# Context row tiles of a PEER layer spread by the steps' times minus the transfer of the weights that they load

## The reference, cut to what matters

```
h  = rmsnorm(x) * (1 + sc1) + sh1
u, v, zb, q, k, rv, rg_f, rg_b, gm = split(h @ w_in)
y_a = gelu(u) * mix128(layernorm(gelu(v)));  y_b = pool(zb) @ pool_w
y_c = silu(rg_f) * headnorm(scan_f(q,k,rv)) + silu(rg_b) * headnorm(scan_b(q,k,rv))
x  = x + gt1 * ((ga*y_a + gb*y_b + gc*y_c) @ w_out)
h2 = rmsnorm(x) * (1 + sc2) + sh2
# PEER: for each token and each of 8 heads, the best 16 of 128 x 128 experts
s1, s2 = (h2 @ wq) . subkeys;  top16 of each side;  top16 of their 256 sums
x  = x + gt2 * sum_experts softmax(score) * gelu(u_tab[e] . h2) * v_tab[e]
y  = rmsnorm(x) * final_norm_g
```

## Time and profile before

| what | value |
|---|---|
| median of 3 runs | 4568.91 us (4568.11 to 4576.76) |
| profiled execution | 4571.26 us, span 4569.5 us |
| TensorE busy, mean granted clock | 3741.4 us (82%), 0.871 |
| VectorE busy | 2791.1 us (61%) |
| DMA | 1672.73 MB, 366 GB/s over the span |
| of it row tiles | 1342.26 MB, 1280 issues |

### The profile page before, as it was taken

How to read it: one execution, slowest core, us unless ns; L and a number is a source line. 1 busy time by engine, 2 the same in 40 slices (tenths; PEclk the granted TensorE clock), 3 DMA queues, 4 the chain that set the end, 5 groups by cost and what they waited for, 6 DMA issues and landing times.

```text
span 4569.5 us, 44582 instructions
## 1 busy us (share of the span) xinstructions
PE 3741.4 (82%) x12065; PEld 1568.4 (34%) x12065; DVE 2791.1 (61%) x6341; ACT 1640.7 (36%) x5133; POOL 1622.7 (36%) x1312
## 2 busy tenths in 40 slices
PE   8999999999998689999776887888777556666666
PEld 6654455656553233443221232342222111011110
DVE  1122776577676976654898566545678984544544
ACT  4211345232213343334344333333343553333333
POOL 0000132223222333333434434443444445555554
PEclk9999999999999799999887998999877676666666
DMA  8645688789999989999999989999999999999998
GB/s 343 228 166 214 261 336 324 272 305 378 373 406 401 366 353 402 382 377 411 398 394 340 420 350 405 400 400 409 401 400 383 395 397 415 413 421 415 415 421 349
DMA packets 277883, 1672.73 MB, mean 366 GB/s; under 512 B 30528, under 2 KB 48000, under 8 KB 91136
## 3 DMA queue, kind: packets, MB, share of 16 engines
q0 software_dynamic: 184320, 1342.26, 73.3%
q1 hardware_dynamic: 85152, 304.18, 17.3%
q10 hardware_dynamic: 8160, 23.43, 1.6%
HBM read 1631.98 MB, written 37.78 MB: 365 GB/s over the span
## 4 chain that ended last, share of the span: by engine, by line
PE 44%; DMA 29%; DVE 14%; issue 7%; ACT 4%; POOL 2%; DVEq 0%; ACTq 0%; SPq 0%; POOLq 0%
DMA slots<-in_peer,idxR 27%; PE ps L1394 27%; PE ps L1412 9%; DVE slots L1701 4%; PE ps L1387 4%; POOL slots L1098 2%; ACT lhs L1153 1%; ACT wgts L1145 1%; DVE ti L1721 1%; DVE ti L1718 1%; DMA counts<-in_mlat 1%; DVE tv L1720 1%; PE ps L1518 1%; DVE rest L1719 1%; ACT gelus L1142 1%
## 5 line engine op out<-in xcount | busy, mean ns | idle before, releaser
L1098 POOL DMA_INDIRECT slots<-in_peer,idxR x1280 | 1616.4, 1263 | 2871.8 <-PE ps L1412 1779.8
L1412 PE MATMUL ps<-slots,lhs 128*64 128x512 f32 x4544 | 1483.1, 767 | 725.2 <-ACT lhs L1153 722.7
L1701 DVE CUSTOM_DVE_ANT_0 slots<-slots,h2R 128x1024 f32<-128x1024 f32 x1280 | 1546.2, 1223 | 763.8 <-issue 706.5
L1394 PE MATMUL ps<-ring,arena 128*128 128x512 f32 (+1 forms) x3264 | 1365.1, 575 | 15.2 <-ACT arena L1353 6.5
L1412 PEld LDWEIGHTS ps<-slots,lhs 128*64 128x64 f32 x4544 | 294.8, 158 | 1811.2 <-ACT lhs L1153 1582.3
L1394 PEld LDWEIGHTS ps<-ring,arena 128*128 128x128 f32 x3264 | 623.2, 195 | 769.8 <-issue 752.3
L1142 ACT ACTIVATE gelus<-dots 128x1 f32<-128x1 f32 x1280 | 256.5, 200 | 1509.6 <-DVE dots L1701 1505.5
L1153 ACT ACTIVATE lhs<-fold,wgts 128x64 f32<-128x64 f32 x1136 | 395.1, 348 | 37.2
L1145 ACT ACTIVATE wgts<-gelus,gsmR 128x1 f32<-128x1 f32 x1280 | 377.2, 295 | 42.4 <-ACT gelus L1142 0.5
L1394 PE MATMUL ps<-ring,slots 128*128 128x512 f32 (+1 forms) x576 | 221.6, 545 | 0.0
L1713 DVE SCALAR_TENSOR_TENSOR slots<-slots,wgts 128x1024 f32<-128x1024 f32 x135 | 172.9, 1281 | 79.0 <-ACT wgts L1145 73.0
(11 more groups left out here) (206 smaller groups left out, 2420.2 us busy)
## 6 DMA issues: line engine op xcount, KB each, us to landing
ring<-in_whead SPq DMA_DIRECT2D x48, 1024.0 KB, 9.6
ring<-in_wa SPq DMA_DIRECT2D x48, 1024.0 KB, 9.2
ring<-in_wq SPq DMA_DIRECT2D x32, 1024.0 KB, 16.2
slots<-in_peer,idxR POOLq DMA_INDIRECT x1280, 13.1
ring<-in_wgc SPq DMA_DIRECT2D x16, 1024.0 KB, 9.5
ring<-in_wgb SPq DMA_DIRECT2D x16, 1024.0 KB, 9.9
ring<-in_wout SPq DMA_DIRECT2D x16, 1024.0 KB, 14.8
o_scratch<-inb SPq DMA_DIRECT2D x80, 128.0 KB, 5.2
```

Of the source, the lines that this page charges most:

```text
L1098: g.indirect_dma_start(out=slot(R), out_offset=None, in_=a["peer"], in_offset=bass.IndirectOffsetOnAxis(ap=idxR[:, p % KEEP, g2, col:col + ...
L1394: done = mm(out, lhsT, rhs, start=n == 0, stop=n == KD - 1)
L1412: done = mm(ps[j * HALF:(j + 1) * HALF, g2, :], weights, slot(R)[:, D + j * UW:D + (j + 1) * UW], start=start, stop=stop)
L1701: v.tensor_tensor_reduce(out=u, in0=u, in1=h2R[:, g2, :], scale=1.0, scalar=0.0, op0=ALU.mult, op1=ALU.add, accum_out=dots[:, R % LHS:R % ...
```

## The change

The weight by which the context's rows (k = 0) are spread is no longer `wall` but `wall` minus 5.3 for each step that starts a weight unit. Groups 1 and 2 keep `wall`, group 3 keeps `spare_time`. The costs of the steps, their order and the number of rows are as before; the rows' places between the steps change, and with them the first row of the chained runs and the row `few` at which slots 6 and 7 come into use.

```diff
         spare = self.spare_time()
+        free = [time - UNIT_TIME * ev.first for time, ev in zip(wall, self.front)]
         due = [0.0] * (len(self.front) + 1)
         for k, cs in enumerate(GROUPS):
             a, b = starts[k], starts[k + 1]
-            weight = spare if k == len(GROUPS) - 1 else wall
+            weight = spare if k == len(GROUPS) - 1 else free if k == 0 else wall
             total = sum(weight[a:b])
             rows = min(len(cs) * ROWS, total / ROW_TIME if k == len(GROUPS) - 1 else len(cs) * ROWS)
```

## The result

The changed kernel takes 4597.62 us (median of 4 runs, 4596.29 to 4605.19) against 4568.51 us before: 29 us more, ratio 1.0067 (95% interval 1.0053 to 1.0080). The forecast was 4566, the range 4552 to 4585: it is wrong, and in the direction of its third rival, which had given 4583.5.

A forecast was written before the change was run, and what follows sets the result against it. It took TensorE to bound most stretches ahead of group 1, VectorE head 3's scans, with DMA near full in group 1; +13.7 ahead and -16.9 in group 1 and after gave -3.2, so 4566 us, range 4552 to 4585.

The forecast's parts named there:

- Rival 3: VectorE becomes the bound ahead of group 1, in ranking, first scans and pools: +14.6 us, 4583.5; chance 0.20.
- Term (a): Ranking: seven more rows at TensorE's 0.98 us, VectorE's cost hidden, +1 for slot refill; 6.8 to 12.1 us.
- Term (d): Scans of head 3: two more rows at 2.5 us, less 2.1 for an eviction moved ahead; +3, 0 to +6.
- Term (g): Group 1's mix and first head gates: chain ends move away, taking 9 of 10 us off; at least 4.
- Term (i): Group 1's transposes and wout: one row fewer saves 1 us (0 to 5); the 4.12 us chain-end wait stays.
- (b): Projections of head 2: 8 rows on TensorE become 10, with no cover; +1.9 us.
- (c): First scan steps of head 2: chained rows, their wait and low clock go, seven TensorE rows come; 0, -2 to +4.
- (f): Group 1's v, u and ga: TensorE is busy 87.93 of 88.2 us, so nothing is saved; 0.
- (h): Group 1's gb: 30.2 us against group 0's 27.4, 0.9 of it a chain end; saves 1.9 (0 to 1.9).
- (j): Query steps of group 1: two rows fewer save 4 us, between 2.0 at TensorE's pace and 5.3 at the DMA engines'.
- (e): Pools: three more rows on VectorE, hidden, and one more chain end on TensorE; +1 us, 7.5 if none hidden.
- Rival 2: Transfers hold back all of group 1, so fewer rows there gain more: -12.5 us, 4556; chance 0.25.

The follow-up runs named there:

- experiment 4: Changed kernel with the dot products of rows 0 to 81 over 512 instead of 1024 elements; 4578.61 us, ratio 1.0028.
- experiment 14: Kernel before with the dot products of rows 0 to 74 over 512 instead of 1024 elements; 4556.58 us, ratio 0.9975.
- experiment 12: Changed kernel with five instead of six slots for the rows up to the end of the ranking; 4608.82 us, ratio 1.0087.
- Experiment 9: Kernel before with 8 rows fewer in the scans of heads 2 and 3 and as many more in the pools; 4570.39 us, ratio 1.0011.
- experiment 10: Kernel before with 63 instead of 75 context rows beside the ranking, the others moved beside heads 2 and 3; 4563.59 us, ratio 0.9992.
- experiment 15: Changed kernel's spread with at most one row in all but one scan step of head 3; 4572.39 us, ratio 1.0014.
- experiment 16: Kernel before with 63 rows beside the ranking, four chain ends taken one row later, and single rows in head 3's scan steps; 4555.88 us, ratio 0.9970.
- experiment 8: Changed kernel with TensorE taking chain ends 175, 191, 207 and 223 one row later; 4587.07 us, ratio 1.0045.
- experiment 6: Kernel before, gathering only the v half of rows 168 to 228, those beside group 1; 4561.83 us, ratio 0.9992.
- experiment 7: Kernel before with TensorE taking chain ends 175, 191, 207 and 223 one row later; 4566.77 us, ratio 0.9999.

## Why the prediction was wrong

**The placement was right, the cost ahead of group 1 was not.** The 60 records, the run that goes back, seven rows beside the ranking and three each beside the later parts all came as worked out (the places from the planner's costs, the records from the trace). The sum ahead of group 1 was +13.7 and is +28 (19.0 ranking, 4.2 head 2, 6.9 head 3, -2 pools); in the second profile it is +32.

**Term (a) failed, by 11 to 13 us.** "VectorE pays 1.30 a row, but is busy 212 of 267 us, which hides it" took an average over two kinds of steps and called its 55 idle us cover. They were none: 17.0 of them are waits for TensorE in the scans between, 19.6 waits for rows to land, and in the ranking's first part VectorE was 94% busy, 67.74 of 72.4 us. What the runs showed in place of the cover: 19.0 to 20.6 us for seven rows, of which 9 to 10 go when half of the dot products is left out on both sides (experiments 4 and 14), and TensorE's idle time in the ranking rises from 11.5 to 20.9 us. Even my upper bound, 12.1, was too low. It charged each row with VectorE's 1.30; it left out that TensorE's wait is followed by slow matmuls (8.76 us for 7.13) and that the six slots come free later, as experiment 12 suggests. Measured, a row is 1.09 us from 63 to 75 rows and 2.7 to 2.9 from 75 to 82. The busy share of the first part alone does not tell the two apart: with 63 rows it is 94% as well (62.86 of 66.7 us). The price of a row is not a constant, and my bounds used one on each side.

**Rival 3 was the right mechanism, with its price too low.** It named the ranking and gave "VectorE's work in a ranking step passes TensorE's 9.8 us" as the point. It had 0.20 because of the "55 us idle", the same average. Its price for the ranking, 12.1, is 8 us below what came; its prices for the first scans and the pools (4 and 7.5) were not paid.

**Term (d): the direction and cause were right, the unit was wrong.** I priced each row that a scan step holds at 2.5 us, less 2.1 for an eviction. Experiment 9 took rows out of head 3's scan steps and gained 0.9, and 4.9 in head 2 where it took away the step with two; experiments 10, 15 and 16 show that a second row in a step is what costs: the wait of 3.51 us and the pair of matmuls at 1.16 us behind it. Three such steps where there had been one gave 6.2 to 8.2; one, as before, gave 0.4.

**Not priced: later scans of head 2 (+3.4) and projections of head 3 (+1).** My list of stretches had a gap from 854.8 to 931.3 us, and what stands there had no term.

**Term (g) was right, and the step behind it missing.** What it said of the two chain ends, "both away from the four evictions of mix", held: -10.0 for -9, and the 6.57 us wait is gone. That the next chain end would land at "the third head gate" was in the text as part of the gain. It cost 6 of the 7 us there: VectorE's last accumulation now stands behind the gate's work and TensorE's use of it one row later, behind the same step. Experiment 8 separates them and has the part at +1.1. I had left the stretch from 1297.2 to 1352.4 out of the sum because before it had no wait.

**Term (i) was wrong in sign, +4 to +9 for -2.** A chain end was foreseen ("a wait of 4.12 us for a chain end stays"); it is 2.71 us. Not foreseen was the wait of 4.85 us, 1.70 before, for an evacuation that now stands behind a table load and a row's gelu. Projections behind these waits take 9.33 and 10.08 us where a clock at full gives some 7.1. The two profiles differ by 5 us here because the clock fell behind the wait of 2.71 in one and not in the other; the size is open to that extent.

**Right: (b), (c), (f), (h), (j).** +2.1 for 1.9, -1.3 for 0, 0 for 0, -2.7 for -1.9, -3.8 and -2.4 for -4. In (c) the mechanism held as well: no wait and no low clock, 20.1 us, all of it busy. The pools (e) gave -2.0 for +1. The carry behind row 256 held within what two profiles of one kernel differ by (3022.7 and 3031.2 around 3025.3).

**Rival 2 and the rule of turns between queues.** Halving the bytes beside group 1 (experiment 6) brought 4.1 us, not the 23.2 of "transfers hold back all of group 1". So rival 2 fell. The forecast had also worked out, from the turns between queues in "DMA: Bandwidth & Descriptors" of the Trainium skill, section "Queues, rings and completion order", that a weight transfer is as late with 47 rows as with 61. That fell too. Group 1's weights in the second profile of the changed kernel (KB each, median us to landing), and one of them before:

```profile
ring<-in_wgb SPq DMA_DIRECT2D x4, 1024.0 KB, 8.2
ring<-in_wout SPq DMA_DIRECT2D x4, 1024.0 KB, 11.4
...
ring<-in_wgb SPq DMA_DIRECT2D x4, 1024.0 KB, 14.3
```

Half of wgb lands in 8.2 us for 14.3, half of wout in 11.4 for 19.1, a row tile in 8.3 for 11.5; only wa is nearly the same, 9.8 for 10.1. Turns as such are not refuted by this, for with fewer rows the rows' queue may be empty more often; no run shows that. In line with it, with 61 rows TensorE came to unlanded weights once the chain ends were late (experiment 7, 2.27 us at the gc weights), with 47 rows it did not (experiment 8). Fewer rows beside a group do bring weights in time; between these two experiments it is 9 us' worth.

**The sum.** Forecast +13.7 - 16.9 = -3.2; measured +28 and +32 ahead of group 1 (first and second profile) and -0.4 and -3.0 in it and its query steps. The corrections, in the first profile: 11.2 for the ranking, 3.2 for head 3's scans, 4.1 for the parts without a term, 7 for the chain end in the remaining head gates and 11 for wout, less 1 to 3 each for the pools, head 2's first steps, mix and gb; -3.2 + 36.5 - 6 is +27, within a microsecond of what was measured (+27.7). The sum closes because its terms are differences between the same two profiles; it shows where the time went, not why.

## What to carry to other kernels

A busy share over a long stretch can hide a full engine: cut the stretch where the kind of step changes, and ask of an engine's idle time what it waits for before counting on it as cover (79% over the ranking was 94% in its first part). The share warns and does not give the price; two points on either side of the planned one do, and halving the engine's work in both kernels shows how much of the price is its own. On an engine that works in order, price what is put between two steps by the step, not by the stretch: in a scan step the first row was nearly free, the second cost its wait and the slow clock behind it. When a spread changes, follow each pair of dependent instructions (a chain's last accumulation and its use) to its new place, also in stretches that had no wait before.

## What the runs showed of the hardware

A wait of 2.7 to 4.9 us on TensorE mostly cost more than itself. A group of 16 float32 matmuls of 128x512 took 7.06 to 7.13 us in the ranking and 8.76 behind a wait of 3.47, 9.33 behind one of 2.71 and 10.08 behind one of 4.85; the granted clock of these stretches is 0.96 and 0.84, between the two levels of 1.2 and 2.4 GHz. So a wait for a chain end that reads as 4.25 us made its part 6 longer than the kernels without it (+7.0 for +1.1). But it was not so every time: the wait of 2.71 us in wout was followed by 9.33 us in one profile and by 7.13 in the other of the same kernel, and one of 3.51 us in head 3 by a pair of matmuls at 0.67 us in the first profile and 1.19 in the second.

For this reason in good part two profiles of one kernel differ by up to 5 us in one part of 60 us (transposes and wout) and by 2 elsewhere, with the first context row reached between 516 and 523 us in all profiles. A smaller difference between two kernels in one part shows nothing by itself.

A DMA share near 1 did not mean that bytes set the pace: group 1 took 266.5 us at a share of 0.82 and 270.8 at 1.00. With 47 row tiles beside group 1 in place of 61, a row tile took 8.3 us (median) to land and not 11.5, and half of wout 11.4 and not 19.1.
